# Transposing attention rows by three 128-partition block transposes and SBUF to SBUF transfers

## What is computed

```python
proj = u @ w_in                       # q | k | v | z, each 2048 wide
logits = q_blk @ k.T * scale + rel_bias        # causal, per head
p = softmax(logits)
a = p[:, :, 0] - lam * p[:, :, 1]     # one row matrix per pair of heads
o = rms_norm(a @ v, subln_g) * (1.0 - lam_init)
y = (o * silu(z)) @ w_out
h = layer_norm(alpha * x + y, g, b)
```

## Time and profile before

| | us |
|---|---|
| median of 3 runs | 942.16 (942.15 to 942.18) |
| span of the profiled execution | 941.2 |
| PE busy | 935.1 |
| DVE busy | 613.9 |
| ACT busy | 325.6 |
| DMA queue of SP | 93.60 MB, 29.6% of the 16 engines |

### The profile page before, as it was taken

How to read it: one execution, slowest core, us unless ns; L and a number is a source line. 1 busy time by engine, 2 the same in 40 slices (tenths; PEclk the granted TensorE clock), 3 DMA queues, 4 the chain that set the end, 5 groups by cost and what they waited for, 6 DMA issues and landing times.

```text
span 941.2 us, 11707 instructions
## 1 busy us (share of the span) xinstructions
PE 935.1 (99%) x4202; PEld 778.2 (83%) x4202; DVE 613.9 (65%) x1195; ACT 325.6 (35%) x590; POOL 64.1 (7%) x140
## 2 busy tenths in 40 slices
PE   9999999999999999999999999999999999999997
PEld 8888888888888888888888888888888888888886
DVE  5545974687468746874687468746874799524466
ACT  4423433333333333433343334333333453222311
POOL 1200010001000100010001000100010000000033
PEclk9999999999999999999999999999999999999999
DMA  8732242224222422242215221422142222742433
GB/s 313 270 100 80 68 163 91 89 67 162 89 89 67 162 89 89 67 162 89 89 67 162 89 89 67 162 89 89 67 134 89 89 67 69 277 158 90 157 103 121
DMA packets 34087, 108.88 MB, mean 116 GB/s; under 512 B 4352, under 2 KB 6400, under 8 KB 33808
## 3 DMA queue, kind: packets, MB, share of 16 engines
q1 hardware_dynamic: 28320, 93.60, 29.6%
q0 software_dynamic: 2336, 9.48, 3.0%
q10 hardware_dynamic: 3408, 5.51, 1.8%
HBM read 104.34 MB, written 9.48 MB: 121 GB/s over the span
## 4 chain that ended last, share of the span: by engine, by line
PE 99%; DMA 0%; DVE 0%; issue 0%; ACT 0%; SPq 0%; DVEq 0%; ACTq 0%
PE proj L1017 79%; PE att L1017 20%; DMA w_raw<-w_in_tiles_dram 0%; DVE big L1009 0%; DVE last_stats L995 0%; ACT bias L660 0%; SPq L326 0%; DVE w_split L865 0%; DVE mean_var L998 0%; DVEq L997 0%; ACTq L659 0%
## 5 line engine op out<-in xcount | busy, mean ns | idle before, releaser
L1017 PE MATMUL proj<-w_split,xg_split 128*128 128x512 f32 x1680 | 385.2, 389 | 0.0
L1017 PEld LDWEIGHTS proj<-w_split,xg_split 128*128 128x128 f32 x1680 | 314.8, 188 | 65.2
L1017 PE MATMUL proj<-xg_split,w_split 128*128 128x512 f32 x1536 | 353.8, 390 | 0.1
L1017 PEld LDWEIGHTS proj<-xg_split,w_split 128*128 128x128 f32 x1536 | 288.0, 188 | 59.6 <-issue 0.3
L464 ACT ACTIVATE w_split<-w_raw 128x1024 fp32r<-128x1024 f32 x128 | 135.8, 1061 | 349.4 <-PE proj L1017 321.1
L681 DVE TENSOR_TENSOR w_split<-w_raw,w_split 128x1024 fp32r<-128x1024 f32 x128 | 155.9, 1223 | 119.4 <-ACT w_split L464 117.8
L759 DVE STREAM_TRANSPOSE scratch<-scratch 32x192 f32<-32x192 f32 (+2 forms) x384 | 141.8, 369 | 5.2
L1017 PE MATMUL att<-w_split,xg_split 128*128 128x512 f32 x432 | 99.9, 389 | 0.0
L1017 PEld LDWEIGHTS att<-w_split,xg_split 128*128 128x128 f32 x432 | 81.0, 188 | 16.8
L942 DVE TENSOR_TENSOR w_split<-w_raw,w_split 128x1024 fp32r<-128x1024 f32 x25 | 30.4, 1223 | 50.9 <-ACT w_split L624 50.9
L425 POOL TENSOR_SCALAR mean_sq<-sq_sum 128x1 f32<-128x1 f32 x32 | 10.3, 322 | 709.3 <-ACT scratch L516 708.0
(11 more groups left out here) (119 smaller groups left out, 465.5 us busy)
## 6 DMA issues: line engine op xcount, KB each, us to landing
w_raw<-w_in_tiles_dram SPq DMA_DIRECT2D x126, 512.0 KB, 3.3
w_raw<-w_out_tiles_dram SPq DMA_DIRECT2D x32, 512.0 KB, 3.3
bias_by_distance<-bias_lines POOLq DMA_DIRECT2D x8, 640.0 KB, 5.0
bias<-bias_by_distance POOLq DMA_DIRECT2D x8, 512.0 KB, 4.0
x_res<-in_x_dram ACTq DMA_DIRECT2D x4, 1024.0 KB, 6.0
big<-x_cols_dram SPq DMA_DIRECT2D x7, 512.0 KB, 8.7
out_dram<-big SPq DMA_DIRECT2D x10, 256.0 KB, 2.5
w_raw<-w_in_tiles_dram SPq DMA_DIRECT2D x4, 256.0 KB, 5.1
```

The costliest lines, as they stand in the source:

```text
L1017: return nc.tensor.matmul(dst, lhsT, rhs, start=start, stop=stop, skip_group_check=True)
```

## The change

`turn` no longer makes 16 instructions. It is one transpose instruction over 128 partitions, which transposes every 32x32 block in place of its own partitions and writes to a buffer `blocks` (the half of `x_res` that nothing else uses during the pairs). What is missing is to move block (i, j) from partition group i to group j. SP does this with 16 transfers per group (`swap_blocks`), each of 32 partitions with one contiguous run of 768 bytes (early), 512 (late) or 1024 (gated), so 24, 16 or 32 KB. The three groups of pair p-1 (0 early, 1 late, 2 gated) stand in SP's queue of pair p behind load 4, load 6 and load 11; those of the last pair stand among the loads of the output weights. All transfers of a group add to `aT_done` or `nT_done`, and the readers wait for the whole group (SWAP = 256 counts). DVE has new waits, because `blocks` is reused: each transpose waits for the transfers of the group before it. `copy_low` waits for the transpose alone (`a_turned`). The transposed buffers have a new order of columns: the outer index is the block within 128 keys, so ACT's and DVE's copies read them with one more dimension. `sq_junk` moves to other columns of `scratch`.

```diff
--- before.py
+++ after.py
@@ -55,6 +55,7 @@
 RING = 4
 LEAD = RING - 1
 B = 32
+NB = P // B
 A_TILES = ST * (ST + 1) // 2
 A_EARLY = A_TILES - ST
 NC = 512
@@ -104,20 +105,21 @@
 
         scratch = sb("scratch", [P, 2 * D])
         logits = scratch[:, 0:1024].rearrange("p (h s) -> p h s", h=2)
-        aT_late = scratch[:, 0:ST * P].rearrange("p (n c) -> p n c", n=ST)
-        gT = scratch[:, 0:1024].rearrange("p (t e c) -> p t e c", t=ST, e=2)
+        aT_late = scratch[:, 0:ST * P].rearrange("p (b x) -> p b x", b=NB)
+        gT = scratch[:, 0:1024].rearrange("p (b x) -> p b x", b=NB)
         silu_z = scratch[:, 1024:2048].rearrange("p (t e) -> p t e", t=ST)
         a_rows = scratch[:, 2048:2048 + A_TILES * P].rearrange("p (n c) -> p n c", n=A_TILES)
         gated = scratch[:, 2048:3072].rearrange("p (t e) -> p t e", t=ST)
-        sq_junk = [scratch[:, 3072 + i * PW:3072 + (i + 1) * PW] for i in range(2)]
+        sq_junk = [scratch[:, 512 + i * PW:512 + (i + 1) * PW] for i in range(2)]
         gated_tiles = scratch[:, 2048:3072].rearrange("p (t e c) -> p t e c", t=ST, e=2)
-        aT_early = scratch[:, 3328:3328 + A_EARLY * P].rearrange("p (n c) -> p n c", n=A_EARLY)
+        aT_early = scratch[:, 3328:3328 + A_EARLY * P].rearrange("p (b x) -> p b x", b=NB)
         lam_vecs = scratch[:, 1024:1024 + 4 * HD].rearrange("p (i n) -> p i n", i=4)
         lam_prod = scratch[:, 1536:1536 + 2 * HD].rearrange("p (i n) -> p i n", i=2)
         bias_line = scratch[0:16, 2048:2048 + BIAS_W]
         ln_g_all, ln_b_all = scratch[:, 0:D], scratch[:, D:2 * D]
         bias = sb("bias", [P, 2, SEQ])
         x_res = sb("x_res", [P, ST, NC])
+        blocks = x_res[:, 2:4].rearrange("p a b -> p (a b)")
         z_rows = x_res[:, 0:2].rearrange("p a (b e) -> p (a b) e", e=PW)
         ident = sb("ident", [P, P])
         table = sb("table", [16, BUCKETS])
@@ -236,6 +238,7 @@
         inv_ready = sem("inv_ready")
         mix_ready = sem("mix_ready")
         a_ready = sem("a_ready")
+        a_turned = sem("a_turned")
         aT_done = sem("aT_done")
         aT_hi = sem("aT_hi")
         aT_ready = sem("aT_ready")
@@ -247,6 +250,7 @@
         rms_ready = sem("rms_ready")
         o_scale_ready = sem("o_scale_ready")
         gated_ready = sem("gated_ready")
+        gated_turned = sem("gated_turned")
         nT_done = sem("nT_done")
         g_ready = sem("g_ready")
         g_hi = sem("g_hi")
@@ -280,9 +284,17 @@
 
             return slice(t * (t + 1) // 2, (t + 1) * (t + 2) // 2)
 
+        def by_tile(turned):
+
+            return turned.rearrange("p b (n c) -> p n b c", c=B)
+
         def turned_a(t):
 
-            return aT_late if t == ST - 1 else aT_early[:, a_tiles(t)]
+            return by_tile(aT_late) if t == ST - 1 else by_tile(aT_early)[:, a_tiles(t)]
+
+        def split_a(t, part):
+
+            return aT[:, t % 2, part, 0:(t + 1) * P].rearrange("p (n b c) -> p n b c", b=NB, c=B)
 
         def x_unit_of(k):
 
@@ -341,6 +353,17 @@
                 sp.wait_ge(w_ready, n - RING + 1)
                 sp.dma_start(w_raw[:, ring(n)], w_out_tiles[tile * P:(tile + 1) * P, :]
                              ).then_inc(raw_loaded[ring(n)], 16)
+
+            def swap_blocks(p, k):
+
+                turned, done, dst = ((a_turned, aT_done, aT_early), (a_turned, aT_done, aT_late),
+                                     (gated_turned, nT_done, gT))[k]
+                sp.wait_ge(turned, p + 1 if k == 2 else 2 * p + k + 1)
+                n = dst.shape[2]
+                for i in range(NB):
+                    for j in range(NB):
+                        sp.dma_start(dst[j * B:(j + 1) * B, i], blocks[i * B:(i + 1) * B, j * n:(j + 1) * n]
+                                     ).then_inc(done, 16)
 
             load_x(0)
             sp.dma_start(w_raw[:, 0, 0:2 * PW], w_in_tiles[0:P, 0:2 * PW]).then_inc(first_loaded, 16)
@@ -370,9 +393,13 @@
             with sp.Fori(1, PAIRS) as p:
                 for j in range(QUARTERS):
                     load_in(p, j)
+                    if j in SWAP_STEPS:
+                        swap_blocks(p - 1, SWAP_STEPS[j])
             for c in range(CHUNKS):
                 for i in range(OQ):
                     load_out(c, i)
+                    if c * OQ + i in SWAP_STEPS:
+                        swap_blocks(PAIRS - 1, SWAP_STEPS[c * OQ + i])
                 if c == 1:
 
                     sp.wait_ge(g_ready, PAIRS)
@@ -500,14 +527,13 @@
             def aT_split(p, t):
                 if not (first_pair(p) and t < 2):
                     act.wait_ge(av_done, p * ST + t - 1)
-                act.wait_ge(aT_done, 2 * p + (1 if t < ST - 1 else 2))
-                nc.scalar.activation(aT[:, t % 2, 0, 0:(t + 1) * P], turned_a(t).rearrange("p n c -> p (n c)"),
-                                     ACT.Copy).then_inc(aT_hi, 1)
+                act.wait_ge(aT_done, SWAP * (2 * p + (1 if t < ST - 1 else 2)))
+                nc.scalar.activation(split_a(t, 0), turned_a(t), ACT.Copy).then_inc(aT_hi, 1)
 
             def copy_low(p, t):
 
                 if t == 0:
-                    act.wait_ge(aT_done, 2 * p + 2)
+                    act.wait_ge(a_turned, 2 * p + 2)
                 act.wait_ge(av_done, p * ST + t + 1)
                 nc.scalar.activation(gated[:, t], av[:, t % 2, 1], ACT.Copy).then_inc(low_copied, 1)
 
@@ -518,10 +544,11 @@
 
             def g_copy(p):
 
-                act.wait_ge(nT_done, p + 1)
+                act.wait_ge(nT_done, SWAP * (p + 1))
                 for e in range(2):
                     dst = g[:, bass.ds(p * 2 + e, 1)]
-                    last = nc.scalar.activation(dst.rearrange("p k (t s) -> p (k t) s", t=ST), gT[:, :, e], ACT.Copy,
+                    last = nc.scalar.activation(dst.rearrange("p k (t b c) -> p (k t) b c", t=ST, b=NB),
+                                                gT.rearrange("p b (t e c) -> p t e b c", t=ST, e=2)[:, :, e], ACT.Copy,
                                                 scale=sub_g[:, e:e + 1])
                 last.then_inc(g_ready, 1)
 
@@ -752,36 +779,36 @@
                                                logits[:, 1, cols], mix[:],
                                                logits[:, 0, cols], ALU.mult, ALU.add).then_inc(a_ready, 1)
 
-            def turn(dst, src):
-
-                for i in range(P // B):
-                    for j in range(P // B):
-                        last = nc.vector.transpose(dst[j * B:(j + 1) * B, ..., i * B:(i + 1) * B],
-                                                   src[i * B:(i + 1) * B, ..., j * B:(j + 1) * B])
-                return last
+            def turn(src):
+
+                n = src.shape[1]
+                return nc.vector.transpose(blocks[:, 0:n * P].rearrange("p (b n c) -> p n b c", b=NB, c=B),
+                                           src.rearrange("p n (b c) -> p n b c", b=NB))
 
             def turn_a_early(p):
 
                 dve.wait_ge(a_ready, p * ST + ST - 1)
                 if not first_pair(p):
                     dve.wait_ge(aT_ready, p * ST)
-                turn(aT_early, a_rows[:, 0:A_EARLY]).then_inc(aT_done, 1)
+                    dve.wait_ge(nT_done, SWAP * p)
+                turn(a_rows[:, 0:A_EARLY]).then_inc(a_turned, 1)
 
             def turn_a_late(p):
 
                 dve.wait_ge(a_ready, p * ST + ST)
-                turn(aT_late, a_rows[:, A_EARLY:A_TILES]).then_inc(aT_done, 1)
+                dve.wait_ge(aT_done, SWAP * (2 * p + 1))
+                turn(a_rows[:, A_EARLY:A_TILES]).then_inc(a_turned, 1)
 
             def turn_gated(p):
 
                 dve.wait_ge(gated_ready, p * ST + ST)
-                turn(gT, gated_tiles).then_inc(nT_done, 1)
+                dve.wait_ge(aT_done, SWAP * (2 * p + 2))
+                turn(gated_tiles.rearrange("p t e c -> p (t e) c")).then_inc(gated_turned, 1)
 
             def aT_split(p, t):
                 dve.wait_ge(aT_hi, p * ST + t + 1)
-                cols = slice(0, (t + 1) * P)
-                nc.vector.tensor_tensor(aT[:, t % 2, 1, cols], turned_a(t).rearrange("p n c -> p (n c)"),
-                                        aT[:, t % 2, 0, cols].bitcast(F32), ALU.subtract).then_inc(aT_ready, 1)
+                nc.vector.tensor_tensor(split_a(t, 1), turned_a(t), split_a(t, 0).bitcast(F32),
+                                        ALU.subtract).then_inc(aT_ready, 1)
 
             def add_low(p, t):
 
@@ -1226,6 +1253,8 @@
                 mm(bank, diag, ln_g_all[:, cols], False, True).then_inc(mean_taken, 1)
 
 
+SWAP = 16 * NB * NB
+SWAP_STEPS = {4: 0, 6: 1, 11: 2}
 AV_STEPS = {0: (0, 1), 3: (2, 3)}
 LAST = PAIRS * QUARTERS + (CHUNKS - 1) * OQ
 OUT_ORDER = [(c, i) for c in range(CHUNKS) for i in range(OQ)]
```

## The result

The changed kernel takes 978.35 us (median of 4 runs, 974.50 to 979.52) beside 942.17 for the kernel before: a ratio of 1.0373, interval 1.0360 to 1.0387. It is 36 us slower where the prediction had 5.4 us slower, and lies outside its range. Slower was right, the place was right, the size was wrong by a factor of over six.

The account below looks back on a forecast made before the run. TensorE was taken as the only bound, busy 935.1 of 941.2 us. Early-group stalls of 6 x 0.40 + 0.67 + 2.34 = 5.4 us, plus 1.0 us around the span, gave 947.6 us, range 943.0 to 958.8.

Parts of the forecast that it names:

- What bounds the kernel, and where it breaks: TensorE, busy 935.1 of 941.2 us; stalls before first quarters, pair 0's weigh_v and the output product.
- Block transposes: Three VectorE instructions a pair over 128 partitions: early 0.97 us, late 0.70, gated 1.24.
- rival 3: Block transpose runs four 32-partition groups in turn, 2.4 us more: X counts as 11.4, time 966.8 us; chance 0.05.
- Landing: Time from a transfer's issue to its data's arrival: 1.9 us for 24 KB, possibly as high as 3.3.
- rival 2: Last transfers queue behind loads and land in 3.3 us: X = 10.43, 958.8 us; chance 0.20 for 952 and above.
- The issue: SyncE's 16 back-to-back transfer issues per group: 0.475 us each, lower bound 0.378, up to 1.68 with queues full.
- X: Cost of a transfer group from SyncE's pickup, 15 issues plus one landing: 9.03 us, bounds 7.57 and 10.43.
- rival 1: Not slower: issues at 0.378 us pitch, X = 7.57, only pair 7 loses 0.88 us, time 943.0; chance 0.19.
- The limits: Largest X without TensorE stall in the early group: 8.63 us (pairs 1 to 6), 8.36 (pair 0), 6.69 (pair 7).
- The clock: TensorE's granted clock read as 1.00 in both windows; stalls counted at their own length, no term for a fall.
- Late group and SyncE's queue: Late data 4.9 us later, covered by ScalarE's 5.96 us idle; weight loads slip up to 7 us; no cost.
- Gated group: Data ready 3.2 us later, covered in pairs 0 to 6; in pair 7 no cost with 2.6 us in hand.

Follow-up runs that it names:

- reorder: Changed kernel with the splits of tiles 0 and 1's transposed rows moved behind the v and z copies on ScalarE and VectorE; 944.36 us (1.0024).
- probe: Kernel before plus 48 extra SyncE DMAs of 512-byte rows in pair 0, six groups of eight, one form of memory ends and rows each; 950.59 us, single run.
- n12: Changed kernel with 12 early-group transfers instead of 16, the four diagonal blocks transposed straight into place by VectorE; 949.28 us (1.0064).
- n8: Changed kernel with 8 early-group transfers instead of 16, the other 8 blocks transposed straight into place by VectorE; 943.73 us (1.0012).
- warm: Changed kernel with ten useless matmuls on TensorE in front of the first quarter of pairs 2 to 7; 971.94 us (1.0305).
- early_only: Changed kernel with late and gated groups back to 16 direct VectorE transposes each, only the early group by block transpose and transfers; 979.08 us (1.0376).
- two_q: Changed kernel with 8 of the early group's 16 transfers issued by ScalarE and 8 by SyncE; 958.79 us (1.0167).
- rest_only: Changed kernel with the early group back to 16 VectorE transposes, late and gated groups by block transpose and transfers; 943.51 us (1.0005).
- hold3: Kernel before with three useless ScalarE copies in front of each pair's v and z copies; 951.14 us (1.0089).
- hold5: Kernel before with five useless ScalarE copies in front of each pair's v and z copies; 982.94 us (1.0420).

## Why the prediction was wrong

**What bounds the kernel, and where it breaks: right.** TensorE as the only bound, no gain from VectorE's 118 us, and the eight idle times are at the places named. `reorder` shows the mechanism as the prediction told it: ScalarE's order, not the rows.

**Block transposes: right.** 0.97, 0.70 and 1.25 us, predicted 0.97, 0.70, 1.24; 128 partitions cost what 32 do (rival 3 falls). **Landing: right**, 1.8 us in the median against 1.9; rival 2 falls.

**The issue: wrong, the term that was mis-sized.** The step said 0.475 us a pitch from the earlier trace rows, bounds 0.378 to 0.475 with 1.68 as a far case. It measured 0.63, so X was 11.2 us, above the predicted upper bound of 10.43. I compared the new transfers with the rows by their number of rows, and took "wider" for an upper bound. They differ in another respect, which no row of before shows: all of SyncE's DMAs there have one end in HBM. `probe` puts the difference on that: 0.591 against 0.422 us. The lower-bound reasoning (rival 1) erred to the same side. The rival whose numbers came nearest, rival 3 (X as 11.4, 966.8 us), has a mechanism that did not happen: the early transpose took 0.97 us, not 3.4.

**The limits: right.** Put into the prediction's own sum, X = 11.23 gives 6 x 2.60 + 2.87 + 4.54 = 23.0 us of idle time; the trace has 22.2. The middle pairs idle 2.37 (2.60 worked out), pair 0 2.96 (2.87), the output product 4.48 (4.54). `n12` and `n8` confirm the limits from the other side. The one that is off is pair 1, 2.89: there one of the 16 issues took 1.11 us instead of 0.59. So with the right X the prediction's sum would have given 942.2 + 23.0 = 965.2 us, still 13 short of 978.35.

**The clock: wrong, a term put at nothing without a reason.** The prediction priced an idle microsecond at a microsecond. The five slow stretches of the profiled execution cost 7.3 - 5.74 = 1.6 us each, 8 us, most of the 9.1 that TensorE's busy time grew. `warm` is 6.4 us faster in the median: its trace has none of the four slow stretches at the gaps that it fills, and one in pair 0 that the trace of the changed kernel does not have. The longer runs of the changed kernel (span 977.7, clock 0.986) have no trace. `early_only`, with the same clock and a span of 977.8, had six slow stretches in eight, two of them of 8.1 and 8.4 us. So of the 36 us some 22 are idle time, and most of the other 13 the clock; that split is read from one execution and not shown for the median one. The second error rests on the first: at 2.2 us more in X the middle pairs went from 0.4 us of idle time each to 2.4, and behind idle times up to 0.50 us no trace has a slow stretch (`two_q`).

**Late group and SyncE's queue: right** (`rest_only`). **Gated group: right for this kernel, in part by luck.** Its 2.6 us in hand were worked out for the smaller X and leaned on TensorE being 2.3 us late. With X = 11.3 and TensorE on time they are gone, and TensorE waits for the last pair's g: 0.75 us in `rest_only` and `n8`, 1.28 in `reorder`. In the changed kernel the stall of 4.48 us before the output product made TensorE late by then, which hid it. The load issues behind the groups were late by up to 10 us and nobody waited for them; `probe` shows that this cover has an end.

Two slips in the working change nothing: pair 0's T is written as 88.00 + 0.97 + 9.03, which gives 98.00; the 98.03 used is 87.94 + 0.97 + 0.09 + 9.03. And the late group's data come 0.70 + 0.09 + 9.03 = 9.8 us after the start, not 9.9.

What stays open: why pair 1's early group meets a slow issue or landing and the later pairs' don't; why idle times of equal length are followed by a slow stretch in some pairs and not in others of one execution; and the rest, 0.6 and 0.5 us, of what `reorder` and `n8` stay above the kernel before.

## What to carry to other kernels

Before a step is moved from an engine to a string of transfers, count issues times the issue price of exactly that form, and find out what stands behind the waiting reader in its engine's order: a reader put behind the urgent copies can wait for free, one in front of them can't. Where the trace has no row with the same two memories at its ends, an issue price from another pair of memories is not a bound. And price an idle time of TensorE by what the clock does behind it. In the kernel before a pair takes 94.2 us. With 1.03 us of idle time it takes 95.5 (`hold3`); with 2.37 us 96.9 where the clock held and 98.5 where it fell.

## What the runs showed of the hardware

- Back to back, a DMA takes 0.59 us of the issuing queue (0.63 pitch; SyncE and ScalarE) if both ends are in SBUF, and 0.42 (0.47; SyncE) if one is in HBM, at 32 or 128 rows of 512 bytes (`probe`) and at 16 to 32 KB in the change. A weight load from HBM right behind a group within SBUF takes 0.58 to 0.59 too. Two queues issued at once for 2.7 us and both kept their 0.63.
- From issue to landing a transfer within SBUF of 16 to 32 KB takes 1.8 to 1.9 us in the median, 3.7 at most in the changed kernel.
- A VectorE transpose of 32x32 blocks over 128 partitions of 512, 768 and 1024 elements a row takes 701, 971 and 1246 ns, within 5 ns of what 168 ns and 1.05 ns an element give, the line through the two rows over 32 partitions.
- Behind idle times of TensorE of 1.94 us or more a stretch at a lower granted clock (0.50 to 0.68 in its first 4 us) came in 25 of 31 cases in seven traces, and where a product of 24 matmuls followed it took 7.1 to 8.6 us instead of 5.7. The six without one were 2.96, 2.89 and 2.37 us (changed kernel), 2.36 and 2.37 (`early_only`) and 2.12 (`hold5`). Past the first 20 us of a run, there was none behind idle times of 1.68 us or less (1.68 before the last ten matmuls in every trace, 1.36 in `warm`, 1.29 in `n12`, 1.28 in `reorder`, 1.03 six times in `hold3`).
